# Who makes the one-hots of the second scatter: GpSimd with the gates, VectorE in one plain operation

## The reference, cut to what matters

```python
idx = jnp.take_along_axis(cand_idx.reshape(...), pos, axis=-1)   # expert number, 128 * i + j
gate = jax.nn.softmax(best, axis=-1)

def blk(args):
    xb, ib, gb = args
    u = U[ib]
    hid = jax.nn.gelu(jnp.einsum('td,thkd->thk', xb, u))
    v = Vt[ib]
    return jnp.einsum('thk,thkd->td', gb * hid, v)
```

## Time and profile before

| | |
|---|---|
| median of 3 runs | 2050.98 us |
| the profiled execution | 2056.76 us, span 2055.0 us |
| busy of the span | PE 70%, DVE 78%, ACT 42%, POOL 48% |
| scatter 1 in this execution | 1523.0 to 1564.7 us |
| the dense phase | 1568 to 2042 us |

### The profile page before, as it was taken

One profiled execution on the slowest core, in us unless ns is written; L12 is line 12 of the kernel. 1 busy time (PEld: TensorE's weight loads), 2 busy tenths in 40 slices (PEclk: granted clock), 3 DMA queues, 4 the chain that ended last, 5 costly groups with the idle time before them and its releaser, 6 DMA issues.

```text
span 2055.0 us, 22565 instructions
## 1 busy us (share of the span) xinstructions
PE 1437.8 (70%) x7933; PEld 1251.2 (61%) x7933; DVE 1609.0 (78%) x1995; ACT 868.0 (42%) x1130; POOL 991.2 (48%) x699
## 2 busy tenths in 40 slices
PE   6999999999999999920000001222348999999997
PEld 6987998877888789920000001111237888888886
DVE  5465775555745556789999999977988999999998
ACT  4353433344343444311111226567756444444444
POOL 1002320000000000178888888888888768888782
PEclk9999999999999999965555555555569999999999
DMA  5555434444555554789999999999955999999996
GB/s 206 185 185 184 163 124 144 154 144 164 184 184 190 199 185 164 266 352 411 421 422 412 415 402 410 414 421 412 421 220 186 390 386 390 393 406 393 394 388 229
DMA packets 151803, 601.81 MB, mean 293 GB/s; under 512 B 14720, under 2 KB 14736, under 8 KB 118288
## 3 DMA queue, kind: packets, MB, share of 16 engines
q0 software_dynamic: 58048, 364.41, 43.8%
q1 hardware_dynamic: 93648, 236.02, 32.1%
HBM read 598.29 MB, written 2.10 MB: 292 GB/s over the span
## 4 chain that ended last, share of the span: by engine, by line
PE 54%; DVE 17%; issue 13%; POOL 7%; DMA 6%; ACT 2%; SPq 0%; DVEq 0%; POOLq 0%; ACTq 0%
PE acc L1706 7%; PE acc L1708 7%; DVE slots L1461 7%; PE acc L1707 7%; POOL slots L536 5%; PE acc L1689 4%; PE acc L1691 4%; PE acc L1692 4%; DMA v_raw<-in_v_dense 3%; PE acc L2012 3%; PE scr L2013 3%; PE acc L2013 3%; PE scr L2012 3%; PE scr L2014 3%; PE acc L2014 3%
## 5 line engine op out<-in xcount | busy, mean ns | idle before, releaser
L942 DVE TENSOR_TENSOR w_lo<-raw,w_hi 128x2048 fp32r<-128x2048 f32 x136 | 314.7, 2315 | 284.5 <-ACT w_hi L597 283.4
L1461 DVE SCALAR_TENSOR_TENSOR slots<-slots,acc 128x2048 f32<-128x2048 f32 x188 | 424.6, 2285 | 46.0 <-DMA slots<-in_peer_u,expert 43.8
L597 ACT ACTIVATE w_hi<-raw 128x2048 fp32r<-128x2048 f32 x136 | 260.1, 1913 | 409.5 <-PE acc L1708 267.2
L581 POOL DMA_INDIRECT starts<-in_v_gather,expert x256 | 360.1, 1407 | 93.8 <-DVE X L1611 80.0
L536 POOL DMA_INDIRECT slots<-in_peer_u,expert x256 | 250.2, 977 | 244.7 <-DVE expert L1433 145.2
L544 POOL TENSOR_TENSOR slots<-slots,N 128x2048 f32<-128x2048 f32 x62 | 280.6, 4525 | 38.8 <-DMA slots<-in_peer_u,expert 38.6
L878 ACT ACTIVATE v_hi<-v_raw 128x1344 fp32r<-128x1344 f32 x128 | 170.5, 1332 | 264.1 <-PE scr L2014 194.3
L791 ACT ACTIVATE slots<-slots 128x2048 f32<-128x2048 f32 x62 | 118.4, 1910 | 342.3 <-POOL slots L544 342.3
L1969 PE MATMUL scr<-hot_a,hot_b 128*128 128x128 f32 x448 | 92.5, 372 | 222.2 <-DVE hot_b L1506 158.5
L1611 DVE SCALAR_TENSOR_TENSOR X<-starts,weight,X 128x704 f32<-128x704 f32 x256 | 242.2, 946 | 3.7 <-DMA starts<-in_v_gather,expert 3.4
L1706 PE MATMUL acc<-w_hi,hT_hi 128*128 128x512 f32 x576 | 227.6, 395 | 2.5 <-DVE w_lo L942 2.5
(11 more groups left out here) (297 smaller groups left out, 3113.8 us busy)
## 6 DMA issues: line engine op xcount, KB each, us to landing
raw<-in_w_in SPq DMA_DIRECT2D x88, 1024.0 KB, 4.9
v_raw<-in_v_dense SPq DMA_DIRECT2D x128, 672.0 KB, 7.5
raw<-in_w_o SPq DMA_DIRECT2D x16, 1024.0 KB, 5.1
raw<-in_peer_wq SPq DMA_DIRECT2D x16, 1024.0 KB, 5.1
raw<-in_w_a_up SPq DMA_DIRECT2D x8, 1024.0 KB, 5.1
raw<-in_w_b_up SPq DMA_DIRECT2D x8, 1024.0 KB, 5.0
slots<-in_peer_u,expert POOLq DMA_INDIRECT x256, 9.6
starts<-in_v_gather,expert POOLq DMA_INDIRECT x256, 8.1
```

What stands on the lines that cost most here:

```text
L581: pool.indirect_dma_start(starts[j][:, :], None, v_gather[:, :], bass.IndirectOffsetOnAxis(ap=expert[:, s // NSEL, s % NSEL:s % NSEL + 1], ...
L597: a.activation(w_hi[:, m % 2, :, :], raw[:, m % 2, :, :], ACT.Copy).then_inc(hi_ready, 1)
L942: v.tensor_tensor(w_lo[:, m % 2, :, :], raw[:, m % 2, :, :], w_hi[:, m % 2, :, :].bitcast(fp32), ALU.subtract).then_inc(lo_ready, 1)
L1461: v.scalar_tensor_tensor(out=slots[j][:, :], in0=slots[j][:, :], scalar=1.0, in1=row, op0=ALU.mult, op1=ALU.mult, accum_out=hid_sum[:, t, ...
```

## The change

For batch 16 and later of scatter 1, the weights move from the second ones to the first ones. GpSimd's `tensor_scalar` gets a second scalar operand and multiplies; VectorE's second ones become one `tensor_tensor` of 128x512 that compares, without weights. Of the first ones of 16 to 31, batches 18, 22, 26 and 30 are now VectorE's, also as one plain 128x512 comparison; there the weights stay in the second ones, as before, in four operations. ScalarE makes none of 16 to 31 any more, GpSimd makes 12 (was 14). GpSimd waits for `gateT` before batch 16.

```diff
 def maker(n):
-    return "act" if n < 12 or n % RING == 3 and n >= PLACES else "pool"
+    if n < 12:
+        return "act"
+    return "dve" if n >= PLACES and n % FOUR == 2 else "pool"
+
+def weighted_first(n):
+    return n >= PLACES and maker(n) == "pool"
...
                     if n >= PLACES:
+                        if n == PLACES:
+                            pool.wait_ge(gateT_ready, 2)
                         pool.wait_ge(hot_used, 2 + BATCHES + last_in_place(n) + 1)
...
-                        last = g.tensor_scalar(hot_a1[place(n)][:, c, :], iota_p, ijT[:, 1, 0, n * SC + c:n * SC + c + 1],
-                                               None, ALU.is_equal)
+                        token = slice(n * SC + c, n * SC + c + 1)
+                        to, row = hot_a1[place(n)][:, c, :], ijT[:, 1, 0, token]
+                        if weighted_first(n):
+                            last = g.tensor_scalar(to, iota_p, row, gateT[:, 1, token], ALU.is_equal, ALU.mult)
+                        else:
+                            last = g.tensor_scalar(to, iota_p, row, None, ALU.is_equal)
...
+            def ones(to, t, c, n):
+                return v.tensor_tensor(to, (iota_p if t else iota_ps).unsqueeze(1).to_broadcast([P, SC, P]),
+                                       ijT[:, t, c, n * SC:(n + 1) * SC].unsqueeze(2).to_broadcast([P, SC, P]),
+                                       ALU.is_equal)
+
             def hot_second(t, n):
+                if t and maker(n) == "dve":
+                    dve.wait_ge(hot_used, 2 + BATCHES + last_in_place(n) + 1)
+                    ones(hot_a1[n % RING][:, :, :], 1, 0, n).then_inc(a_ready[3], 1)
                 dve.wait_ge(hot_used, max(2 + BATCHES, BATCHES + n) if t else 1 + n)
                 to = hot_b1[n % 3] if t else hot_b[:, n % 2, :, :]
-                if t == 0 and n < ACT_WEIGHTS:
+                if weighted_first(n) if t else n < ACT_WEIGHTS:
+                    ones(to, t, 1, n).then_inc(b_hot_ready, 1)
                     return
```

More of the change, by code:

```diff
@@ L391, in build @@
         a_one, a_dist, a_ready, b_hot_ready, hot_used, scattered = (
-            sem("a_one"), sem("a_dist"), [sem("a_ready0"), sem("a_ready1_pool"), sem("a_ready1_act")], sem("b_hot_ready"), sem("hot_used"), sem("scattered"))
+            sem("a_one"), sem("a_dist"), [sem("a_ready0"), sem("a_ready1_pool"), sem("a_ready1_act"), sem("a_ready1_dve")], sem("b_hot_ready"), sem("hot_used"), sem("scattered"))
         start_landed = [sem(f"start_landed{j}") for j in range(2 * CRING)]
@@ L1499, in _ @@
             link(v.tensor_copy(iota16_ps, iota16[:, :]))
+            def ones(to, t, c, n):
+                return v.tensor_tensor(to, (iota_p if t else iota_ps).unsqueeze(1).to_broadcast([P, SC, P]),
+                                       ijT[:, t, c, n * SC:(n + 1) * SC].unsqueeze(2).to_broadcast([P, SC, P]),
+                                       ALU.is_equal)
             def hot_second(t, n):
+                if t and maker(n) == "dve":
+                    dve.wait_ge(hot_used, 2 + BATCHES + last_in_place(n) + 1)
+                    ones(hot_a1[n % RING][:, :, :], 1, 0, n).then_inc(a_ready[3], 1)
                 dve.wait_ge(hot_used, max(2 + BATCHES, BATCHES + n) if t else 1 + n)
                 to = hot_b1[n % 3] if t else hot_b[:, n % 2, :, :]
-                if t == 0 and n < ACT_WEIGHTS:
-                    v.tensor_tensor(to, iota_ps.unsqueeze(1).to_broadcast([P, SC, P]),
-                                    ijT[:, 0, 1, n * SC:(n + 1) * SC].unsqueeze(2).to_broadcast([P, SC, P]),
-                                    ALU.is_equal).then_inc(b_hot_ready, 1)
+                if weighted_first(n) if t else n < ACT_WEIGHTS:
+                    ones(to, t, 1, n).then_inc(b_hot_ready, 1)
                     return
@@ L1965, in scatter @@
                     by = maker(n)
-                    pe.wait_ge(a_ready[("pool", "act").index(by) + 1], sum(maker(m) == by for m in range(n + 1)))
+                    pe.wait_ge(a_ready[("pool", "act", "dve").index(by) + 1], sum(maker(m) == by for m in range(n + 1)))
                 pe.wait_ge(b_hot_ready, t * BATCHES + 1 + n)
```

## The result

The changed kernel takes 2057.23 us (median of 8 runs, 2054.34 to 2059.7) against 2049.78 (8 runs, 2048.1 to 2053.68) of the kernel before on the same chip: ratio 1.0031, 95% interval 1.0021 to 1.0041, so 6.4 us slower (4.3 to 8.4).

A forecast was written before the change was run, and what follows sets the result against it. GpSimd's operations were taken to bound scatter 1's end, VectorE close behind: batch 24's release 1545.6 + 24 x 0.78 + 1.22 = 1565.5 against 1564.7, +0.8 us. Forecast 2051.8 us, range 2048.0 to 2057.0.

The forecast's parts named there:

- B: Rival, scatter 1: each plain VectorE comparison holds up one GpSimd operation, 0.40 us delay; 7.5 us slower, 2058.5; chance 12%.
- C: Rival, scatter 1: GpSimd's second scalar is dear, 0.3 us, first half ends after the release; 8.7 us slower, 2059.7; chance 9%.
- X: Scatter 1: price of one weighted GpSimd operation, 0.78 us in the second half, 0.72 in the first; break-even 0.746.
- e: GpSimd's operation in scatter 1: time added by second scalar and multiplication, taken as 0.08 us, bounded by 0 and 0.307.
- the copy against the memset: GpSimd rows of 128x1024, 1032 against 955 ns: one more stream read costs 0.077 us, used for the second scalar.
- The upper bound's row: GpSimd compare-and-select without a scalar from memory, 283 ns against 590 with one: a second scalar costs at most 0.307 us.
- The release of batch 24: Scatter 1: stays at 1545.6, since GpSimd makes batches 16 to 23 by 1542.9, before it.
- No clock step is at stake: Scatter 1 and after: TensorE runs at full clock, granted 1.00, 2.4 GHz, so no clock effect was counted.
- Part 1: VectorE from batch 16 on: 14.7 us of work against 17.9 that TensorE needs at 1.12 a batch; VectorE leaves the bound.
- A: Rival, scatter 1: GpSimd's operation still costs 0.641, TensorE's own pace limits; gain 2.5 us at most, 2048.5; chance 22%.
- D: Rival, batches 24 to 31: they wait on TensorE's use of their places, not GpSimd; nothing moves, 2051.0; chance 7%.
- The dense phase as a block that is shifted: Dense phase behind scatter 1: unchanged in length, so what the scatter's end gains or loses, the kernel does.

The follow-up runs named there:

- psum_one_scalar: Changed kernel with the iota row of VectorE's plain comparisons in PSUM and no weight in GpSimd's operations (output lacks these weights): scatter 37.2 us, ratio to before 0.9979.
- psum_ones: Changed kernel with the iota row of VectorE's plain comparisons in PSUM, nothing else changed: scatter 44.8 us, ratio to before 1.0006.
- one_scalar: Changed kernel without the weight in GpSimd's operations of batches 16 to 31 (output lacks these weights): scatter 43.4 us, ratio to before 1.0006.
- mix: Changed kernel with the iota row in PSUM and GpSimd's weights only for batches 16, 17, 20 and 21: scatter 38.4 us, ratio to before 0.9978.
- maker_late: maker_only, with GpSimd waiting until TensorE has used the last batch before its gathers of V: scatter 41.1 us, ratio to before 1.0024.
- before_two_scalars: Kernel before, with the weight as second scalar in GpSimd's operations of batches 16 to 31 (weights applied twice): scatter 52.7 us, ratio to before 1.0041.
- before_times_one: Kernel before, with a multiplication by the constant 1.0 in GpSimd's operations of batches 16 to 31: scatter 48.2 us, ratio to before 1.0013.
- maker_only: Changed kernel with only its moved batches: GpSimd unweighted, all second ones weighted as before; scatter 41.3, 41.3, 41.2 us, ratios to before 0.9981, 0.9985, 0.9992.
- psum_act_two: Changed kernel with the iota row in PSUM and ScalarE keeping the first ones of batches 19 and 27: scatter 38.5 us, ratio to before 0.9985.

## Why the prediction was right and wrong

**Where the bound lies: right.** The scatter's end was to be read from GpSimd, and it is: the end less 1.8 us is its last operation. VectorE left the bound as worked out.

**The number.** A loss of more than 0.2% had a chance of 19%, all of it from B and C. The forecast's own spread of X gave -1.1 to +2.7 us. That the result lies near the end of the range is owed to the room left toward B; no term of the forecast's sum gave it, so in this the range was lucky.

**X, the price of one operation: the term that was mis-sized.** I had 0.581 + 0.08 + 0.12 = 0.78 in the second half and 0.72 in the first; it was 45.63 / 48 = 0.951 over both, and the miss was greater in the first half (1.05) than in the second (0.85). In its parts:

- e, 0.08 by the copy against the memset. The second scalar's read is 0.079, so that row gave the right size. "The multiplication needs none" was wrong: 0.118 us. Together 0.197, which lies inside the bounds of 0 and 0.307. The upper bound's row should have had more weight, since it held a compare without a scalar and the copy held no arithmetic at all.
- The delay by VectorE. A weighted operation alone is 0.776 from start to start, so 48 would take 37.2 us, and 8.4 were added, 0.175 each (that this is the number of the scatter's loss too is chance). Beside the small operations I carried over today's 0.06. But that was a property of the lockstep, two of VectorE's to one of 0.58; with an operation of 0.78 it is three to one, and 0.12: 2.2 us over 18 operations. The plain comparisons from SBUF do what the earlier trace rows showed, and more than once for one operation when several stand in a row (2.56 us). They took the other 6.2 us, 4.4 of them from the six operations behind 1533.80, which still belong to GpSimd's first half. By the forecast the first half ends 19.9 us into the scatter, just as VectorE's first plain comparison begins (20.0). That one began at 18.8, and GpSimd had begun the 19th of its 24.

**The release of batch 24: the step that failed by it.** The sum was release + 24 X + 1.22, with the first half hidden behind TensorE. That holds up to X = 20.0 / 24 = 0.83 in the first half. At 0.90 alone the stop would vanish; with the six slow ones batch 24 was 5.3 us late, and the sum became 2.7 + 48 X + 1.8 = 50.1. A price that I counted for 24 operations was paid for 48. I had seen this shape in rival C, at e = 0.3, and did not look for the point from which it begins, 0.19 above the lockstep's 0.64.

**TensorE's clock: a smaller step that failed.** "No clock step is at stake" was read from the kernel before. With TensorE waiting for GpSimd the granted clock fell, and the last term of the sum was 1.8 us instead of 1.22. The rest of the fall costs nothing here, since GpSimd's 48 operations have no pause.

**Two slips in the working.** With 85 ns in place of 0.08 the sum would rise by 24 x 0.005 = 0.1 us, not 0.2. And the 1.12 us a batch of TensorE in Part 1 and in A was no backlog, as psum_one_scalar shows.

**Rivals.** B and C were both partly right in the cause, and neither in the way: psum_ones takes 5.3 us of the 8.4 away, one_scalar 6.7. B's sign, scattered durations, came true (the longest 1.8 above the shortest, not 0.6), but B left the release of batch 24 where it was; C had the release late, with even durations near 1 us, which were 0.90 in the first 18 and scattered behind them. The rule of the Trainium skill, SBUF — State Buffer, § Who interferes with whom, cited at B, stands: with the iota row in PSUM the comparisons take as long as before (0.68 us) and GpSimd's stalls are gone. The row of 2.56 us goes further than a wait for one comparison: that operation was held through three. A's bound (2.5 us) rested on 1.12 us a batch for TensorE, which is 0.93; psum_one_scalar gains 4.5 in the scatter and 4.3 in the time. That kernel's output lacks weights, but mix, which leaves nothing out, has 3.3 us of it. D is out: GpSimd's 48 operations have no pause at all.

**The dense phase as a block that is shifted: wrong in general, harmless here.** maker_late shows that a microsecond of the gathers' lead can be worth more than a microsecond. In the changed kernel the lead is 1.6 instead of 1.1 us, and the scatter's 8.4 us came out as 6.4, with an interval from 4.3 to 8.4. In the first 30 us behind the scatter TensorE is idle 2.7 us, 3.7 before, which would be 1 us of the difference; that the lead makes the rest isn't shown.

## What to carry to other kernels

When VectorE and GpSimd both read SBUF, the cost of an operation on one depends on what the other does: price them as a pair, keep one of VectorE's two operands in PSUM where a bank has room (the same duration here, and GpSimd is no longer held), and redo the lockstep's arithmetic when either operation gets longer. Before a price is multiplied by a count, look for the slack that hides the other half of the operations, and divide: it gives the price from which that half is no longer free. And an engine that is done early is worth something if transfers stand behind it in its queue; look at what it starts next, not only at who waits for its last result.

## What the runs showed of the hardware

- One GpSimd `tensor_scalar` of 128x128 fp32 with a scalar from memory: 0.590 us; with a multiplication by a constant 0.708; with a second scalar from memory 0.787.
- A GpSimd operation can be held through several VectorE operations in a row: 2.56 us for one of 0.79, behind three comparisons with two SBUF operands each.
- VectorE's 128x512 comparison takes 0.68 to 0.69 us (medians) with its iota row in SBUF or in PSUM alike.
- GpSimd's operation with two scalars, 0.776 us from start to start alone, goes at 0.90 beside VectorE's small `tensor_scalar`, three of them to one; the one with one scalar, 0.58 alone, goes at 0.64, two to one.
- TensorE at full clock does a batch of four 128x128 fp32 products in 0.93 us when everything is ready (psum_one_scalar), and starts one every 1.28 us in the kernel before, where it waits for VectorE each time. Where it idled between batches for 1 to 3 us several times in a row, its granted clock fell to between 0.50 and 0.82 in stretches of 5 us (both profiles of the changed kernel, psum_ones, one_scalar, before_two_scalars, before_times_one); in psum_one_scalar, mix and maker_only, where no wait was longer than 0.7 us, it stayed at 1.00 from 1520 to the scatter's end, and so it did in psum_act_two, which had two waits of 1.1 and 1.3 us.
